# Sample dilated attention by 16 KB key runs and diagonal far queries, with the output projection spread between its key transposes

## The reference

```python
DIL_PATTERNS = ((128, 1), (512, 4), (2048, 16))
...
    n = jnp.arange(window // dil + 1)
    idx = P + jnp.arange(L)[:, None] - dil * n[None, :]
    kg = k_ext[:, idx]
    vg = v_ext[:, idx]
    s = jnp.einsum('bihd,binhd->bhin', q, kg).astype(F32) * (Dh ** -0.5)
    s = s - alibi_slopes()[:, None, None] * (dil * n).astype(F32)
...
    return jnp.concatenate([r, a], axis=-1).astype(dtype) @ w_o
```

## Time and profile before

| | |
|---|---|
| median of 3 runs | 1280.04 us (1275.24 to 1281.36) |
| span of the profiled execution | 1275.2 us |
| the run whose time equals that span | 1275.24 us, the lowest of the three |
| sample attention, 379.5 to 536.5 us | 157 us |
| output projection, 536.5 to 595.8 us | 59.3 us |
| `project_memory` begins | 595.86 us |

### The profile page before, as it was taken

How to read it: one execution, slowest core, us unless ns; L and a number is a source line. 1 busy time by engine, 2 the same in 40 slices (tenths; PEclk the granted TensorE clock), 3 DMA queues, 4 the chain that set the end, 5 groups by cost and what they waited for, 6 DMA issues and landing times. The chain is left out here.

```text
span 1275.2 us, 15545 instructions
## 1 busy us (share of the span) xinstructions
PE 969.1 (76%) x5808; PEld 686.8 (54%) x5808; DVE 545.3 (43%) x879; ACT 351.6 (28%) x615; POOL 119.5 (9%) x142
## 2 busy tenths in 40 slices
PE   3999998777667778497979767769636888888860
PEld 3888887655445555385758666448532333333320
DVE  3574712435665444342645562453263222232224
ACT  4453222001663323333455343233300000000000
POOL 1350000313000000000112300000101000000003
PEclk9999999555698978798979888889766999998885
DMA  7111214201407999762340040783354999999946
GB/s 227 67 67 66 79 54 141 66 5 26 132 22 229 293 261 293 231 256 79 114 150 1 33 166 31 266 298 131 96 205 145 416 422 422 423 422 422 423 196 224
DMA packets 80979, 242.22 MB, mean 190 GB/s; under 512 B 21280, under 2 KB 21920, under 8 KB 66464
## 3 DMA queue, kind: packets, MB, share of 16 engines
q1 hardware_dynamic: 72848, 219.34, 47.7%
q0 software_dynamic: 3616, 13.11, 2.8%
q10 hardware_dynamic: 4464, 9.08, 1.8%
HBM read 218.04 MB, written 23.46 MB: 189 GB/s over the span
## 5 line engine op out<-in xcount | busy, mean ns | idle before, releaser
L1917 PE MATMUL bank<-gate_up,slot_rows_t 128*64 128x512 f32 x512 | 114.9, 600 | 1.5 <-DVE slot_rows_t L1958 0.9
L349 PE MATMUL bank<-in_wh,in_hth 128*128 128x512 f32 x224 | 88.5, 395 | 3.1 <-DVE in_wl L293 3.1
L1934 PE MATMUL bank<-down,hidden_t 128*64 128x512 f32 x256 | 81.9, 798 | 8.3 <-issue 7.3
L350 PE MATMUL bank<-in_wl,in_hth 128*128 128x512 f32 x224 | 87.9, 393 | 0.0
L351 PE MATMUL bank<-in_wh,in_htl 128*128 128x512 f32 x224 | 87.9, 392 | 0.0
L1917 PEld LDWEIGHTS bank<-gate_up,slot_rows_t 128*64 128x64 f32 x512 | 42.7, 139 | 70.8 <-issue 70.8
L1123 PE MATMUL bank<-ident,k_half 128*128 128x128 f32 x320 | 54.0, 319 | 18.4 <-DVE window_k_t L1025 8.2
L1123 PEld LDWEIGHTS bank<-ident,k_half 128*128 128x128 f32 x320 | 41.3, 162 | 30.9 <-DVE window_k_t L1025 15.9
L1934 PEld LDWEIGHTS bank<-down,hidden_t 128*64 128x64 f32 x256 | 26.8, 178 | 52.3 <-issue 52.3
L1964 DVE TENSOR_SCALAR swish<-swish 128x256 f32<-128x256 f32 x16 | 4.7, 294 | 108.8 <-ACT swish L1942 108.8
L349 PEld LDWEIGHTS bank<-in_wh,in_hth 128*128 128x128 f32 x224 | 42.6, 190 | 12.3 <-issue 3.5
(11 more groups left out here) (376 smaller groups left out, 2133.5 us busy)
## 6 DMA issues: line engine op xcount, KB each, us to landing
gate_up<-w_exp_gate SPq DMA_DIRECT2D x32, 1024.0 KB
gate_up<-w_exp_up SPq DMA_DIRECT2D x32, 1024.0 KB
down<-w_exp_down SPq DMA_DIRECT2D x32, 1024.0 KB
in_w<-w_in SPq DMA_DIRECT2D x7, 2048.0 KB, 8.0
k_half<-cache_win_k SPq DMA_DIRECT2D x48, 256.0 KB, 7.1
v_half<-cache_win_v SPq DMA_DIRECT2D x48, 256.0 KB, 5.3
k_half<-cache_win_k SPq DMA_DIRECT2D x8, 1024.0 KB, 10.8
v_half<-cache_win_v SPq DMA_DIRECT2D x8, 1024.0 KB, 9.7
```

The lines of the kernel that those rows point to most:

```text
L349: pe.matmul(o, hi, wh[b % 2][:, c, :], start=(c == 0), stop=False)
L350: pe.matmul(o, hi, wl[b % 2][:, c, :], start=False, stop=False)
L1917: last = pe.matmul(m.bank[2][64 * h:64 * h + 64, :], B.xt[s][:, c, 64 * h:64 * h + 64], B.gu[s][h][:, :, c, :], start=(c == 0), stop=(c == ...
L1934: last = pe.matmul(m.bank[4 + j][64 * h:64 * h + 64, :], B.hidt[s][:, k, 64 * h:64 * h + 64], B.dn[s][h][:, k, 512 * j:512 * j + 512], sta ...
```

## The change

- **Keys and values.** The far rows come in one transfer: 96 partitions, one for each group of 16 positions, with the 8 rows of residues 0 to 7 (16 KB) in each. Near rows come as before, in one transfer. A request takes four transfers in place of 14.
- **Scores.** The far keys are turned residue by residue (8 chunks of 96 keys) and the near keys in 4 chunks of 128. For the far part GpSimd lays the queries out so that the chunk of residue s has the query s in its column and zeros elsewhere. All eight chunks add into the same 96 score columns, so a request has 96 + 512 + 64 = 672 score columns in place of 1344. Likewise each far chunk of values is multiplied by probabilities that are zero but for the query s. A chunk is scored two chunks behind its transpose; the turned keys go through a ring of four.
- **No loops.** The 8 passes are written out.
- **The output projection** has no stage of its own. The 24 matmuls of prompt tile product k are spread over the key pass k+1, two behind each of the first ten key chunks; the last four stand between the transposes of the probabilities and the products with the values. Its row and weight splits are done by ScalarE and VectorE behind the copies of key chunks. VectorE adds the products to `x` from PSUM, without ScalarE's copy. The sample tile follows the last request.
- **Transfers.** The first half of `w_o` is loaded at the end of `mix_prompt`, the second behind the first values. The memory rows and the first weights of `project_memory` are loaded at the end of the stage; the first weights of `project_cross` no longer wait for a product. The zeros are written in `project_cross`, as one transfer.

```diff
-            for is_v, i in ((0, 0), (0, 1), (1, 1)):
-                m.windows.load(sp, 0, is_v, i)
+            m.windows.load_far(sp, 0, 0)
+            m.windows.load_near(sp, 0, 0)
+            m.w_o.load(sp)
...
+        self.far = [c[:, :, 0:WBUF - NEAR].rearrange("a b (g r) h d -> (a b) g r (h d)", r=16) for c in (ck, cv)]
...
+    def load_far(self, sp, b, is_v):
+        dst, sem = (self.vf, self.vf_in) if is_v else (self.kf, self.kf_in)
+        sp.dma_start(dst[:FG], self.far[is_v][b, :, 0:LS, :]).then_inc(sem, 16)
...
+            sp.dma_start(btab[:], a["c_btab"]).then_inc(tab_in, 16)
+            sp.wait_ge(held, 2)
+            win.load_near(sp, 0, 1)
+            win.load_far(sp, 0, 1)
+            w_o.load(sp)
+            for n in range(1, NB):
+                sp.wait_ge(kt_done, WC * (n - 1) + LS)
+                win.load_far(sp, n, 0)
+                sp.wait_ge(kt_done, WC * n)
+                win.load_near(sp, n, 0)
+                if n >= 2:
+                    sp.wait_ge(pv_done, n - 1)
+                    win.load_near(sp, n - 1, 1)
+                    win.load_far(sp, n - 1, 1)
...
+            def keys(n, k):
+                for c in range(WC):
+                    turn_keys(n, c)
+                    if k is not None and c < WC - 2:
+                        wo_part(k, 2 * c, 2 * c + 2)
+                    if c == 1 and n >= 2:
+                        turn_out(n - 2)
+                    if c >= 2 and c % 2 == 0:
+                        score(n, c - 2)
+                        score(n, c - 1)
+                    if c == LS:
+                        score_own(n)
+                score(n, WC - 2)
+                score(n, WC - 1)
...
+            keys(0, None)
+            for n in range(NB):
+                if n + 1 < NB:
+                    keys(n + 1, n)
+                else:
+                    turn_out(n - 1)
+                    wo_part(n, 0, 2 * (WC - 2))
+                turn_probs(n)
+                wo_part(n, 2 * (WC - 2), 3 * C8)
+                products(n)
+            turn_out(NB - 1)
...
+            for n in range(NB):
+                exps(n)
+                if n + 1 < NB:
+                    keys(n + 1, later(n + 1))
+                turned(n)
...
+    def later(sp, mm_done):
+        sp.wait_ge(zero_done, 1)
+        sp.dma_start(m.slots_dram[NPAIR * P:].rearrange("(n p) d -> p n d", p=P), across(zero[:], 1, NOVP)).then_inc(zero_out, 16)
+        sp.wait_ge(zero_out, 16)
...
-        stages = (load_constants, project_in, mix_prompt, mix_windows, project_out, project_memory, project_cross,
+        stages = (load_constants, project_in, mix_prompt, mix_windows, project_memory, project_cross,
```

More of the change, by code:

```diff
@@ L56 @@
 NEAR = 512
[L57 to L60, removed]
+FG = (WBUF - NEAR) // 16
+NC = NEAR // P
+WC = LS + NC
+WK = FG + NEAR + NS
 MEM, MH, MD = 256, 4, 256
@@ L928 @@
 class Windows:
[L931 removed]
     def __init__(self, m, a):
[L934 to L936 removed]
+        self.kf, self.kn = m.at("window_k_far", m.Z, [LS, RW]), m.at("window_k_near", m.Z + 8192, [NC, RW])
+        self.vf, self.vn = m.at("window_v_far", m.Z + 10240, [LS, RW]), m.at("window_v_near", m.Z + 4096, [NC, RW])
@@ L937, in __init__ @@
+        self.kf_in, self.kn_in, self.vf_in, self.vn_in = (m.sem(f"window_{n}_in") for n in ("k_far", "k_near", "v_far", "v_near"))
         ck, cv = a["cache_win_k"], a["cache_win_v"]
-        self.far = [c.rearrange("a b (c g r) h d -> (a b) g r c (h d)", g=16, r=16) for c in (ck, cv)]
+        self.far = [c[:, :, 0:WBUF - NEAR].rearrange("a b (g r) h d -> (a b) g r (h d)", r=16) for c in (ck, cv)]
         self.near = [c[:, :, WBUF - NEAR:].rearrange("a b (p c) h d -> (a b) p c (h d)", p=P) for c in (ck, cv)]
[L941 to L949, removed]
@@ L983, in _ @@
             sp.dma_start(btab[:], a["c_btab"]).then_inc(tab_in, 16)
[L985 to L1002, removed]
@@ new lines, in score @@
+            def score(n, c):
+                i = WC * n + c
+                if c == 0:
+                    pe.wait_ge(q_done, 4 * (n + 1))
+                    if n:
+                        pe.wait_ge(sb_done, 3 * n)
+                pe.wait_ge(kt_ev[c % 2], i // 2 + 1)
+                for q in range(NP):
+                    rows_ = slice(32 * q, 32 * q + 32)
+                    if c < LS:
+                        last = pe.matmul(m.bank[SF][rows_, 0:FG], qd[:, c, rows_], kt[:, i % RING, q, 0:FG], start=(c == 0),
+                                         stop=(c == LS - 1), skip_group_check=True)
+                    else:
+                        last = pe.matmul(m.bank[SN][rows_, full(c - LS)], qb[:, q, :], kt[:, i % RING, q, :], start=True, stop=True,
+                                         skip_group_check=True)
+                last.then_inc(ws_done, 1)
@@ new lines, in turn_probs @@
+            def turn_probs(n):
+                pe.wait_ge(ex_done, n + 1)
+                if n:
+                    pe.wait_ge(pt_near, n)
+                    pe.wait_ge(pt_far, 3 * n)
+                for j in range(NC):
+                    last = pe.transpose(m.bank[PN][:, full(j)], sb[:, FG + j * P:FG + (j + 1) * P], m.ident[:, :])
+                last.then_inc(pt_done, 1)
+                pe.transpose(m.bank[PF][:FG, 0:P], sb[:, 0:FG], m.ident[:, :])
+                pe.transpose(m.bank[PF][:NS, P:2 * P], sb[:, FG + NEAR:WK], m.ident[:, :]).then_inc(pt_done, 1)
@@ L1235, in later @@
     def later(sp, mm_done):
-        for b in range(2):
-            sp.wait_ge(mm_done, 2 * (b + 3))
-            m.w_mq.load(sp)
+        m.w_mq.load(sp)
+        sp.wait_ge(mm_done, 8)
+        m.w_mq.load(sp)
     dense(nc, m, "mem", m.mem_rows, m.w_mem, range(2), store, hooks, m.g_mem, [P, P], m.Z + 10240, arrived, later)
```

485 lines of the change are left out of this document (294 added, 191 removed).

## The result

The changed kernel takes 1264.18 us (median of 18 runs, 1258.16 to 1270.97); the kernel before, run again as often, 1274.55. The ratio is 0.9918 (95% interval 0.9893 to 0.9942): some 10 us faster, where the forecast had 32.5.

The account below looks back on a forecast made before the run. DMA was taken to bound the old attention loop, TensorE the projection. Start to 404.6, seven passes of 18.6 and a tail end the stage at 563.4 instead of 595.86: 32.5 less, 1247.5 us median; range 1224 to 1276.

Parts of the forecast that it names:

- the slow restart: First pass after TensorE's wait at the stage's start: products run at the lower clock, 2 us added.
- I take 276: far 5.7: Far transfers in the new stage: the old kernel's 276 GB/s kept, so 5.7 us for each far transfer.
- the rivals at 0.13: Far loads slower, in all passes: at 200 GB/s total 1270 us; decides below 233 GB/s; chance 0.13.
- 5.1 + 2f: Load chain per request: first data 2.2, near values 2.9, far values and next far keys f each; 16.5 us.
- A request on TensorE: Each pass of the new stage: 18.6 us of TensorE work, bounds 16.3 to 20.9.
- Changes of shape: Scores between transposes in a pass: some 16 changes a request at 0.09 us each, 1.4 in all.
- the rival of shorter passes: Passes: shape changes free and short transposes short, 16.3 us, chain holds at 16.5; total 1231 us; chance 0.17.
- The start: Stage's first issue at 379.47 to second key pass at 402.6, before the 2 us added for the lower clock.
- The tail: After the seventh products at 534.8: last values land at 545.6, next stage begins at 563.4.
- The other engines: VectorE 11.2 us and ScalarE 7.8 us a request, both covered by TensorE's 18.6.
- The clock: Rival, passes at TensorE's lower clock: half the work there gives 1311 us, all of it 1374; chance 0.10.
- Code that is written out: Rival, unrolled passes: 6 to 16 more instruction pieces at 2.2 us uncovered, 13 to 35 us, about 1272; chance 0.08.

Follow-up runs that it names:

- e12: Changed kernel with far transfers on 128 partitions in place of 96, timed in rounds beside it: 1247.68 us, ratio 0.9776.
- e1: Changed kernel with far rows read from 768 consecutive cache rows, still on 96 partitions: 1259.68 us, one run.
- e2: Changed kernel with far transfers bringing 16 KB of all 128 groups to 128 partitions, a third more bytes: 1242.81 us, one run.
- e5: Changed kernel with far transfers on 128 partitions, each cut into eight with 2 KB pieces: 1244.78 us.
- e9: Kernel before the change with far rows read from consecutive addresses, same twelve transfers of 128 rows: 1253.65 us, ratio 0.9825.
- e3: Changed kernel with each far transfer cut into two, 8 KB pieces on the same 96 partitions: 1259.31 us, one run.
- e4: Changed kernel with each far transfer cut into eight, 2 KB pieces on the same 96 partitions: 1246.77 us, one run.
- e10: As e8, but every chunk scored by itself, two chunks behind its transpose, in place of two together: 1240.68 us, ratio 0.9739.
- e6: Changed kernel with the last request's values loaded into the buffers of its keys: 1261.23 us, one run.
- e11: The changed kernel itself, timed a second time: 1265.28 us, ratio 0.9952.
- e8: Changed kernel with far transfers on 128 partitions, last values in key buffers, second half of w_o loaded behind second request's far keys: 1231.97 us, ratio 0.9673.

## Why the prediction was wrong

The three parts of the sum, against the changed kernel and against e12, which differs from it in the partitions of the far transfers alone, and so in a third more of their bytes (us):

| | forecast | changed | e12 |
|---|---|---|---|
| first issue to second key pass | 23.1 | 28.0 | 23.4 |
| seven passes, with the slow restart | 132.2 | 147.2 | 134.2 |
| end of the seventh products to the next stage | 28.6 | 33.2 | 31.2 |
| stage | 183.9 | 208.4 | 188.8 |

**The step that failed** is "I take 276: far 5.7": the far transfers move 228 GB/s and take 6.9 us each. The 276 was read from a row of the old kernel because the new transfer reads the same addresses. e1 shows on 96 partitions that addresses don't set the rate, e2 and e5 that 128 partitions in place of 96 raise it to over 400. Nor was 276 the rate of such rows as such: 2 KB pieces of the same pattern move at 404 in e5, consecutive ones at 418 in e9. What is left for the old figure is the way its transfers laid 16 groups of 8 rows over 128 partitions; that was not tried by itself. I had the mechanism among the rivals at 0.13, with "only 96 partitions take part" named for it, and gave more weight to the row.

**The price of such a rate** was wrong too, in the chain "5.1 + 2f". 228 is below the condition of that rival, "below 233 GB/s", so the rival came in; but by its own terms 228 costs 2.1 us in the passes, 2.4 at the start and 1.2 in the tail, which gives about 1253. Measured are 15.0, 4.9 and 4.6 above the forecast (table), of which 2.0, 0.3 and 2.6 stay in e12. That the price which the rival names, a gain of some 10 us (1270 against 1280.04, worked out at 200 GB/s), is what was measured is luck in part. Nor is 233 the border: at 259 (e3) three passes still wait for far keys, at 267 (e4) none.

The rival had 20.9 us for every pass; the mean is 147.2/7 = 21.0, but in another form. With f at 6.9 the chain is 5.1 + 2 x 6.9 = 18.9, which would leave hardly a wait. From the issue of the near values to TensorE's start on the far keys behind them it took 23.0 (425.61 to 448.61) and 19.9 (512.10 to 532.04); in the first of these the near values alone landed 9.3 us after their issue, in the second 5.3. Why, no run shows. Over the seven passes the time is 15.7 us above 7 x 18.79. Of these, 5.5 are the waits for far keys behind the start (4.28 and 1.21) and 2.9 two pauses (0.88 and 2.01); the 7.3 left are the lower clock behind the start, the longer wait and the longer pause. That 13.0 of the 15.7 hang on the rate of the far loads is shown by e12 (134.2 in place of 147.2); in e2, e4 and e5, too, none of the six passes behind the first products waits for far keys, pauses on "issue" or takes more than 18.8.

That e12's 1247.68 is the forecast's 1247.5 is luck as well: the forecast was counted from 1280.04, the median of three runs, which over 18 runs is 1274.55 and beside e12 1270.86. e12 gains 23.2 of the 32.5. And the sum as told in words (23 back as tail and start, 0.9 more per request) doesn't give 32.5; by the rows it is 8.5 in the start, 9.5 in the tail and 1.3 per request.

Of the rest of the sum:
- **A request on TensorE**, 18.6: right, 18.77 to 18.79 where nothing disturbs it.
- **Changes of shape**, 0.09 each: right, 0.09 by e10 (up to 0.13), and the rival of shorter passes falls with it. The trace agrees with the rule of the Trainium skill that was weighed there, "TensorEngine Tiling (Array Packing)", section "Key Properties", in that a change has a price.
- **The slow restart**, 2 us: about right. In e12 the first pass takes 400.05 to 421.48, 21.4 us with a clock that rises in it, 2.6 above the others.
- **The start**, 23.1: in e12 it is 23.4, though its far loads are 0.7 shorter than I took; the values are issued only 1.4 us behind the table (377.15 against 375.74 in the changed kernel), which I had not counted. The two far transfers at 228 add 3.8 of the 4.6 that the changed kernel's 28.0 is longer.
- **The tail**, 28.6: 2.6 short even in e12. In the changed kernel the last values land 13.6 us after their issue (550.97 to 564.57) in place of 10.8, and the products behind that wait run at the lower clock: 564.57 to 568.54, 4.0 in place of 2.1. I had counted that clock for the sample tile and not for the products.
- **The other engines** never end a wait of length in the passes, as forecast.
- **The clock** as a cause of its own fell: the undisturbed passes are granted 1.00, and in the passes the lower level shows only behind a wait or a pause.
- **Code that is written out**: the queue brings 47 pieces in place of 33, 14 more, within the 6 to 16 of the estimate. Two pauses on "issue", 2.9 us together, stand in the products; in e12, where DMA has idle time, there are none. In the five kernels with disturbed passes (the changed one, e1, e3, e6 and e11) the products hold ten such pauses, and in the records of the traces each ends 1.3 to 1.7 us after a packet of the instruction queue has ended (here packets of 421.57 to 422.96 and 486.95 to 488.31). That speaks for code that arrives late behind data; no edit tested it.

So the large rebuilding gained little because its own load came more slowly than the one it replaced. e9 turns this round: with good loads the old structure gains 18.6 us, the new one 23.2 (e12). 14.2 us a request and 5.44 for a product of the projection are 19.6, and laying the projection into the passes (18.8) saves 0.8 a request more. With the order of its loads and the tail put right as well (e8) the new structure is 41.7 us below the kernel before; what these two would bring in the old structure was not tried, nor were such loads of the reference's own rows there.

The Trainium skill, "SBUF — State Buffer", section "Door 1: The DMA port swizzle (why `[64,N]` ≈ `[32,N]`)", says that the rate of a DMA depends on how many of 16 SBUF ports its partitions reach. By its table partitions 0 to 95 reach all 16 ports, as 0 to 127 do, so this count alone would not tell 228 GB/s on 96 from 422 on 128; the measurement decides. Which port a packet went to no run here shows.

## What to carry to other kernels

When a change alters how a transfer is laid over partitions, the rate of the old transfer is no row for it, even if the addresses are the same: look for a row with the same partitions and piece, or keep both ends of the range open as cases of equal weight. Try a large load on all 128 partitions, even if a quarter of what it brings isn't used. 128 partitions were not enough by themselves, though (276 GB/s in the kernel before), so read the rate of the new load from its own trace. And before two stages are laid on each other, ask whether the one that is bound by DMA could simply be loaded faster.

## What was not expected of the hardware

- More bytes took less time: 2.10 MB on 128 partitions 5.0 us (422 GB/s), 1.57 MB on 96 partitions 6.9 us (228).
- On 96 partitions longer pieces were slower: 267, 259 and 228 GB/s for 2, 8 and 16 KB; on 128 partitions 2 KB gave 404 and 16 KB 422.
- Reading consecutive rows in place of half of every 32 KB changed nothing on 96 partitions: 231 against 228.
